# A router stage re-ordered and halved, a last output in two halves, and two norms whose high halves feed TensorE first

## The reference

```
for i in range(DEPTH):                       # DEPTH = 2
    h = pool_mixer(x, ...) if i % 2 == 0 else nsa_mixer(x, ...)
    x = layer_norm(ALPHA * x + h, ln_g[i, 0], ln_b[i, 0])
    f = swiglu(x, ffn_w_gu, ffn_w_down) if i % 2 == 0 else moe_ffn(x, moe_router, moe_w_gu, moe_w_down)
    x = layer_norm(ALPHA * x + f, ln_g[i, 1], ln_b[i, 1])

def moe_ffn(x, router, w_gu, w_down):        # 8 experts, the best 2 of each token, weights by softmax
    top_v, top_i = lax.top_k(x @ router, 2)
    w = softmax(top_v)
    for e in range(8):
        y = y + combine[:, e:e + 1] * swiglu(x, w_gu[e], w_down[e])
```

## Time and profile before

| | |
|---|---|
| median of 3 executions | 2326.48 us |
| lowest and highest | 2321.36 and 2332.45 us |
| the profiled execution, its own time | 2330.26 us |
| its span in the profile | 2328.3 us |
| mean granted TensorE clock | 0.992 |
| busy: TensorE, VectorE, ScalarE | 98%, 81%, 57% |
| expert 0's first slot begins at | 1322.33 us |
| the last expert's last slot ends at about | 2307.9 us |

### The profile page before, as it was taken

The page is one execution under the profiler, slowest core; times in us unless marked ns, Lnnn a source line. Parts: engine busy times, 40 slices in busy tenths (PEclk is TensorE's granted clock), DMA queues, the critical chain, the costliest instruction groups (busy, mean ns, idle before and its releaser), DMA issues.

```text
span 2328.3 us, 35730 instructions
## 1 busy us (share of the span) xinstructions
PE 2281.9 (98%) x14752; PEld 2055.5 (88%) x14752; DVE 1891.2 (81%) x2054; ACT 1322.5 (57%) x1321; POOL 2.4 (0%) x8
## 2 busy tenths in 40 slices
PE   9999999999999999999999999999999999999998
PEld 9799999989989999999987888888888888888886
DVE  7896987787869978645666779898898989898886
ACT  6544343554444434433436377767776777777775
POOL 0000000000000000000000000000000000000000
PEclk9999999999999999999999899999999999999999
DMA  6343445533434553655330399999999999999996
GB/s 264 109 168 136 169 181 182 186 130 117 167 129 177 181 181 127 229 181 182 124 122 9 120 336 374 358 342 368 359 369 363 345 360 373 358 343 356 374 359 257
DMA packets 169552, 556.75 MB, mean 239 GB/s; under 512 B 8752, under 2 KB 8880, under 8 KB 133168
## 3 DMA queue, kind: packets, MB, share of 16 engines
q1 hardware_dynamic: 168048, 547.44, 64.4%
q10 hardware_dynamic: 1152, 6.50, 0.7%
q0 software_dynamic: 192, 0.52, 0.1%
HBM read 552.86 MB, written 1.05 MB: 238 GB/s over the span
## 4 chain that ended last, share of the span: by engine, by line
PE 88%; DVE 6%; ACT 3%; issue 1%; DMA 1%; ACTq 0%; SPq 0%; DVEq 0%
PE ps L1135 14%; PE ps L1137 14%; PE ps L1136 13%; PE ps L1129 12%; PE ps L1131 12%; PE ps L1130 12%; PE ps L1318 2%; ACT whi L628 1%; DMA raw<-stream 1%; DVE wlo L1973 1%; PE ps L1600 1%; PE ps L1797 1%; PE ps L1340 1%; PE ps L1399 1%; PE ps L1421 1%
## 5 line engine op out<-in xcount | busy, mean ns | idle before, releaser
L1973 DVE TENSOR_TENSOR wlo<-raw,whi 128x2048 fp32r<-128x2048 f32 x513 | 1172.1, 2289 | 238.5 <-ACT whi L628 183.2
L628 ACT ACTIVATE whi<-raw 128x2048 fp32r<-128x2048 f32 x513 | 982.3, 1916 | 540.5 <-PE ps L1131 289.8
L1129 PE MATMUL ps<-hh,whi 128*128 128x256 f32 x1920 | 549.0, 286 | 8.1 <-DVE hl L2156 2.1
L1130 PE MATMUL ps<-hl,whi 128*128 128x256 f32 x1920 | 543.8, 283 | 0.0
L1131 PE MATMUL ps<-hh,wlo 128*128 128x256 f32 x1920 | 543.8, 283 | 0.0
L1135 PE MATMUL ps<-whi,hh 128*128 128x512 f32 x960 | 385.6, 402 | 2.0 <-DVE hl L2913 2.0
L1129 PEld LDWEIGHTS ps<-hh,whi 128*128 128x128 f32 x1920 | 369.0, 192 | 11.6 <-issue 6.9
L1137 PE MATMUL ps<-wlo,hh 128*128 128x512 f32 x960 | 377.3, 393 | 0.0
L1136 PE MATMUL ps<-whi,hl 128*128 128x512 f32 x960 | 376.3, 392 | 0.0
L1130 PEld LDWEIGHTS ps<-hl,whi 128*128 128x128 f32 x1920 | 369.1, 192 | 0.3
L1131 PEld LDWEIGHTS ps<-hh,wlo 128*128 128x128 f32 x1920 | 368.9, 192 | 0.0
(11 more groups left out here) (382 smaller groups left out, 2558.3 us busy)
## 6 DMA issues: line engine op xcount, KB each, us to landing
raw<-stream SPq DMA_DIRECT2D x519, 1024.0 KB, 5.5
work<-w_in ACTq DMA_DIRECT2D x1, 2240.0 KB, 9.8
stage<-stage_consts ACTq DMA_DIRECT2D x4, 512.0 KB, 4.0
work<-mem_in ACTq DMA_DIRECT2D x2, 1024.0 KB, 5.4
x<-x_in SPq DMA_DIRECT2D x1, 1024.0 KB, 5.2
out<-x SPq DMA_DIRECT2D x4, 256.0 KB, 2.3
const<-consts SPq DMA_DIRECT2D x1, 548.5 KB, 12.0
work<-work POOLq DMA_DIRECT2D x4, 128.0 KB, 2.8
```

What stands on the lines that cost most here:

```text
L628: nc.scalar.activation(whi[hi_at(g, odd)][:, :], raw[g % RAWS][:, :], ACT.Copy).then_inc(hi_ready, 1)
L1129: mm(out_ap, hi_w, hi_x, start=start, stop=False, **kw)
L1130: mm(out_ap, hi_w, lo_x, start=False, stop=False, **kw)
L1973: V.tensor_tensor(wlo[g % RAWS][:, :], raw[g % RAWS][:, :], whi[hi_at(g, odd)][:, :].bitcast(F32), ALU.subtract).then_inc(lo_ready[g % RAW ...
```

## The change

**Norms 0 and 1.** VectorE now scales all eight blocks and then makes the eight blocks of `hl`. ScalarE follows block by block. The first slot is a new function, `hi_first_slot`: 6 zero matmuls, the wait for the rstd, 2 zero matmuls in place of 16, then 32 matmuls that need only `hh`, each pair of blocks' four as its block is rounded, and last the 16 that need `hl`. Norms 2 and 3 also hand over by block instead of by quarter.

**Router stage.** VectorE's `split_lo(FIRST + AHEAD)` leaves norm 2 and stands between the two kept halves of the gather. Two of the four count products go, and the maximum is taken over the eight columns of places themselves, whose row 0 holds the totals. 10 zero matmuls stand in place of 16. The gather's results are kept and used by halves: expert 0's r = 0, then its r = 1, then the weight half, then expert 1's. TensorE's slot 0 waits for the first half alone. The last four `take_of`, `expert_weights` and the scaling of x move to slots 2, 4 and 8 of expert 0, and `few_give` with the slots' weights to slots 6 and 10.

**The end.** The last down slot takes its matmuls by output half. The high and low half are written by halves, and the first spread needs only the first. 3 zero matmuls stand between the spreads, where 22 stood ahead of them. The table load goes ahead of the last output, the squares and folds move into the branch, and the second half's squares are summed behind the mean.

```diff
+        GIVE_AT = (6, 10)
...
-                for c in range(QUARTERS):
-                    act.wait_ge(norm_scaled, QUARTERS * (SCALED_AT["ln"] + i) + c + 1)
-                    if last:
-                        with_bias(c, x, x_ready)
-                    else:
-                        with_bias(c, hh, hi_done)
+                for b in range(NB):
+                    act.wait_ge(norm_scaled, scaled_block(i, b))
+                    ins = with_bias(b, x if last else hh)
+                    if not last:
+                        ins.then_inc(hi_done, 1)
+                    elif b % 2:
+                        ins.then_inc(x_ready, 1)
...
+                act.wait_ge(y_half_ready, 1)
+                nc.scalar.activation(FEW_Y_HI[:, 0:512], ps[:, 3, :], ACT.Identity, scale=slot_weight(e)).then_inc(y_hi, 1)
+                act.wait_ge(slot_used, SLOTS)
+                nc.scalar.activation(FEW_Y_HI[:, 512:1024], ps[:, 4, :], ACT.Identity, scale=slot_weight(e)).then_inc(y_hi, 1)
...
-                few_keep_y(EXPERTS - 1)
+                load_log_exp()
+                few_keep_last_y()
+                last_squares()
...
+            def hi_first_slot(ph, i, h):
+                g, bank = ph.g, ph.g % BANKS
+                hi, lo = whi[hi_at(g)], wlo[g % RAWS]
+                wait_lo(pe, g)
+                pe.wait_ge(banks_drained, ph.e - 2)
+                keep_warm(bank, 6)
+                pe.wait_ge(rstd_ready, 9 + i)
+                keep_warm(bank, 2)
+                w = lambda t, b, c: t[:, (b * NB + c) * P:(b * NB + c + 1) * P]
+                to = lambda b: ps[:, bank, b * BLK:(b + 1) * BLK]
+                for c in range(NB):
+                    pe.wait_ge(hi_done, rounded_block(i, c))
+                    x_hi = hh[:, c * BLK:(c + 1) * BLK]
+                    for b in range(2):
+                        mm(to(b), w(hi, b, c), x_hi, start=c == 0 and b == 0, stop=False, skip_group_check=True)
+                        mm(to(b), w(lo, b, c), x_hi, start=False, stop=False, skip_group_check=True)
+                for c in range(NB):
+                    if c % 2 == 0:
+                        pe.wait_ge(h_ready, QUARTERS * (h - 1) + c // 2 + 1)
+                    for b in range(2):
+                        last = mm(to(b), w(hi, b, c), hl[:, c * BLK:(c + 1) * BLK], start=False, stop=c == NB - 1, skip_group_check=True)
...
+                squares_of(0)
                 pe.wait_ge(x_folded, 4)
                 ones_sum(MEAN_BANK[3], FOLDED_X[3], False, True).then_inc(mean_ready, 1)
+                squares_of(1)
...
-            ffn_pe(2, 14, norm=8, idle=16)
+            ffn_pe(2, 14)
...
+            hi_first_slot(PHASES["nsa_in"], 1, 15)
...
-            mm(ps[:, 1, 0:8], C("ones"), ind[:, 8:16], start=False, stop=True, skip_group_check=True)
-            mm(ps[:, 1, 16:24], C("ones"), ind[:, 0:8], start=True, stop=False)
-            last = mm(ps[:, 1, 16:24], C("ones"), ind[:, 8:16], start=False, stop=True)
+            last = mm(ps[:, 1, 0:8], C("ones"), ind[:, 8:16], start=False, stop=True, skip_group_check=True)
             last.then_inc(counts_ps, 1)
-            keep_warm(7, 16)
+            keep_warm(7, 10)
...
+                ends = closes and e == EXPERTS - 1
+                order = [(c, b) for b in range(2) for c in range(2)] if ends else [(c, b) for c in range(2) for b in range(2)]
...
+                    if ends and (c, b) == (1, 0):
+                        last.then_inc(y_half_ready, 1)
...
-                pe.wait_ge(gathered, e + 1)
+                if e:
+                    pe.wait_ge(gathered, e + 2)
...
+                        if e == 0 and part == 0 and s < 2:
+                            pe.wait_ge(gathered, s + 1)
...
-                keep_warm(7, 22)
                 pe.wait_ge(y_kept, EXPERTS)
                 few_spread(EXPERTS - 1, 0, 5)
+                keep_warm(7, 3)
+                pe.wait_ge(y_kept, EXPERTS + 1)
                 few_spread(EXPERTS - 1, 1, 3)
...
-                for c in range(QUARTERS + 1):
-                    if c < QUARTERS:
-                        for b in (2 * c, 2 * c + 1):
-                            ins = V.scalar_tensor_tensor(out=xb(b), in0=xb(b), scalar=R("ln_g", g_at + b), in1=rstd[:, :],
-                                                         op0=ALU.mult, op1=ALU.mult)
-                        ins.then_inc(norm_scaled, 1)
-                    if c and not last:
-                        dve.wait_ge(hi_done, QUARTERS * HI_AT[f"ln{i}"] + c)
-                        for b in (2 * c - 2, 2 * c - 1):
-                            cols = slice(b * BLK, (b + 1) * BLK)
-                            ins = V.scalar_tensor_tensor(out=hl[:, cols], in0=xb(b), scalar=R("ln_b", 8 * i + b), in1=hh[:, cols].bitcast(F32),
-                                                         op0=ALU.add, op1=ALU.subtract)
-                        ins.then_inc(h_ready, 1)
+                for b in range(NB):
+                    V.scalar_tensor_tensor(out=xb(b), in0=xb(b), scalar=R("ln_g", g_at + b), in1=rstd[:, :],
+                                           op0=ALU.mult, op1=ALU.mult).then_inc(norm_scaled, 1)
+                if not last:
+                    for b in range(NB):
+                        dve.wait_ge(hi_done, rounded_block(i, b))
+                        cols = slice(b * BLK, (b + 1) * BLK)
+                        ins = V.scalar_tensor_tensor(out=hl[:, cols], in0=xb(b), scalar=R("ln_b", 8 * i + b), in1=hh[:, cols].bitcast(F32),
+                                                     op0=ALU.add, op1=ALU.subtract)
+                        if b % 2:
+                            ins.then_inc(h_ready, 1)
...
-            layer_norm(2, 16, last=True, beside=FIRST + AHEAD)
+            layer_norm(2, 16, last=True)
...
-            step(V.tensor_reduce(small[:, 472:473], ps[:, 1, 16:24], AX, ALU.max))
+            step(V.tensor_reduce(small[:, 472:473], ps[:, 1, 0:8], AX, ALU.max))
...
-                for odd in range(2):
-                    if odd == 0:
-                        dve.wait_ge(gathered_ps, 1)
-                    first = keep_x_hi(0, odd, 5)
-                    if odd == 0:
-                        dve.wait_ge(gathered_ps, 2)
-                    second = keep_x_hi(1, odd, 3)
-                    keep_x_lo(0, odd, 5, first)
-                    keep_x_lo(1, odd, 3, second).then_inc(gathered, 1)
+                def keep_first(r, odd, done=None):
+                    bank = (5, 3)[r]
+                    dve.wait_ge(gathered_ps, r + 1)
+                    lo = keep_x_lo(r, odd, bank, keep_x_hi(r, odd, bank))
+                    if done is not None:
+                        lo.then_inc(done, 1)
+                keep_first(0, 0, gathered)
+                keep_first(1, 0, gathered)
+                split_lo(FIRST + AHEAD)
+                keep_first(0, 1)
+                keep_first(1, 1, gathered)
                 V.memset(small[:, 639:640], 0.0).then_inc(gather_kept, 2)
-                for n in range(12, 16):
-                    ins = take_of(n)
-                ins.then_inc(places_built, 1)
-                V.tensor_scalar(x[:, :], x[:, :], ALPHA, None, ALU.mult).then_inc(y_added, 1)
-                expert_weights()
+                def last_takes():
+                    for n in range(12, 16):
+                        ins = take_of(n)
+                    ins.then_inc(places_built, 1)
+                def scale_x():
+                    V.tensor_scalar(x[:, :], x[:, :], ALPHA, None, ALU.mult).then_inc(y_added, 1)
+                beside_first = {2: last_takes, 4: expert_weights, 8: scale_x}
...
-                few_keep_y_lo(EXPERTS - 1)
+                for half in range(2):
+                    cols = slice(512 * half, 512 * (half + 1))
+                    dve.wait_ge(y_hi, EXPERTS + half)
+                    V.scalar_tensor_tensor(out=FEW_Y_LO[:, cols], in0=ps[:, 3 + half, :], scalar=slot_weight(EXPERTS - 1),
+                                           in1=FEW_Y_HI[:, cols].bitcast(F32), op0=ALU.mult, op1=ALU.subtract).then_inc(y_kept, 1)
...
+                last_folds()
```

91 lines of the change are left out of this document (51 added, 40 removed).

## The result

The changed kernel took 2313.15 us, the median of 8 executions (2311.34 to 2315.35). The kernel before took 2327.81 us beside it (8 executions, 2321.36 to 2334.0). The ratio is 0.9944, with a 95% interval of 0.993 to 0.9959. That is 14.7 us or 0.56% faster, and the interval reaches across the line of 0.5%. A later set of 7 executions of the same changed kernel gave 2313.74 us and a ratio of 0.9952 (0.993 to 0.9973). The forecast was 2315.0 us.

What follows compares the result with a forecast made beforehand. TensorE, busy 2281.9 of 2328.3 us, was taken as the bound; 3.8 + 5.9 + 1.7 - 1.0 + 3.1 + 0.4 = 13.9 us gave 2316.4 from the profile, 2313.4 from the median, middle 2315.0; range 2309 to 2323 us.

Steps and rivals of the forecast that it cites:

- norms 0 and 1: First slots behind both norms: TensorE starts on the first rounded block and ends 1.9 us earlier each, together 3.8 us.
- slot 0 of expert 0, behind norm 2's rstd: Router stage: earlier gather, then no wait for conversions, so slot 0 starts at 1316.4 in place of 1322.33, 5.9 us.
- clock behind the pause: Stretch 1320 to 1330, behind the 1.98 us pause: without a pause the 1.2 GHz loss goes, 1.7 us.
- the wait for `routed`: Expert 0, ahead of the column products: VectorE's moved work ends late and TensorE waits, -1.0 us.
- the end, with norm 3 by block: Behind the last slot: mean at 2314.35 in place of 2317.45, 3.1 us, and norm 3's hand-over by block another 0.4 us.
- Rival (d): Norms 0 and 1: first slots still end with the last `hl` and gain nothing, 2318.8 us; chance 0.05.
- The gather's start: Router stage: the gather starts at 1311.8 in place of 1315.85, 4.05 us, behind VectorE's flag, low half and takes.
- rival (c): Around the gather: the low clock also gets shorter, up to another 3 us won, 2312 us; chance 0.08.
- rival (b): Expert 0: VectorE's queue runs late, up to 6.4 us less won, 2321.4 us; chance 0.10.
- The prediction's own alternative: At the end: were the instruction fetch stall behind the branch twice as long, the 3.1 us would be 2.0.
- Rival (a): Norms 0 and 1: TensorE's pauses bring 1.2 GHz stretches; one fall gives 2316.7 us, both 2318.4; chance 0.30.
- Rival (e): Norms, router and end: long 1.2 GHz stretches cost 20.9 us, slower than before at 2335.9 us; chance 0.02.

Runs made afterwards that it cites:

- the end alone: The kernel before with only the change's part at the end (output halves, 3 zeros, table load, folds and squares in the branch): 2324.09 us, ratio 0.9996.
- its own run: The changed kernel with the low weight half made at the end of norm 2 again, as in the kernel before: 2316.94 us.
- the norms alone: The kernel before with only the norms' part (high halves first behind norms 0 and 1, hand-over by block in all four norms): 2323.95 us, ratio 0.998.
- the gather whole: The changed kernel with the gathered x kept as before, slot 0 of expert 0 waiting for both halves: 2314.23 us.
- the router part alone: The kernel before with only the router stage's part (weight half, counts, zeros, gather by halves, moved work): 2320.55 us, ratio 0.9976.
- The run with the norm in the branch: The changed kernel with norm 3 of VectorE and ScalarE written inside both branches of the experts: 2313.28 us, ratio 0.9958.

## Why the prediction was right, point by point

The forecast of 2315.0 us is 1.9 us above the first median and 1.3 above the second. 11.6 us (0.5%) was the line between faster and no change. The medians lie 3.1 and 1.1 us past it, but both intervals reach back across it, so the measurement leaves open which of the two it is; the prediction had given 0.40 to faster and 0.58 to no change.

| step | forecast, us | profile before to profile after, us |
|---|---|---|
| norms 0 and 1 | 3.8 | 1.88 + 1.87 = 3.75 |
| slot 0 of expert 0, behind norm 2's rstd | 5.9 | 22.40 - 15.82 = 6.6 |
| clock behind the pause, less the wait for `routed` | 1.7 - 1.0 = 0.7 | slot 0 to last slot 985.5 - 983.2 = 2.3 |
| the end, with norm 3 by block | 3.1 + 0.4 = 3.5 | 20.47 - 17.91 = 2.6 |
| places that the change leaves alone | 0 | norm 1 to norm 2's rstd 3.2, ahead of norm 0 0.5 |
| sum | 13.9 | 18.9 |

- **Norms: right, with its mechanism.** First matmul 1.54 us behind the rstd (1.4 forecast); the part alone gives the same. Rival (d) falls.
- **The gather's start: the changed row as forecast, the gain (4.02 us against 4.05) in part by luck.** Logits' end to gather is 6.22 us, the forecast 6.3. But the forecast set this against rows of before that were partly at 1.2 GHz (1.73 us for the count products and 3.76 us for 16 zeros, at a clock of 0.65), as if they were the kernel's own. Against the same stage with the same 1.7 us lost (the end alone) the gain is 2.25 us: the weight half's (1.7 to 2.4 us by its own run) and norm 2's hand-over by block (0.3 to 0.4). The other 1.8 us are clock: before lost 1.6 + 3.5 us from 1300 to 1320, after 0.6 + 1.1 us from 1290 to 1310. The cut products and zeros bring nothing at the full clock. The forecast had TensorE's zeros (1311.5) and VectorE's takes (1311.8) nearly level; VectorE comes 0.93 us later.
- **Slot 0: the mechanism right, its size too large.** No idle time there; from the first transpose 10.28 us (10.9 forecast, 16.5 before), and the halves give 2.1 us by their own run. The gather takes 3.92 us and not 4.6, at a higher clock. But at equal lost time the stage gains 4.4 us, not 5.9 (4.1 if the 16.12 of the changed kernel's second profile is taken, which lost 1.7 us there too); the 6.6 of the table has 2.2 us of clock in it. This is rival (c) in part: it had the low clock get shorter.
- **The stretch behind the pause of 1.98 us** was gone, but it need not have been there. The pause stood in four profiles (before, the norms alone, the end alone, the gather whole), and only before had the clock fall right behind it. Of the 2.3 us in the table 1.7 are the clock (3.4 us lost in before from slot 0 on, 1.7 in after), and the rest goes with TensorE's waits in the experts, which come to 3.5 us in before and 2.7 in after.
- **`routed`: oversized.** 0.24 us in after (0.47 with the router part alone), not 1.0. No wait for a weight half stood in expert 0, so rival (b) falls.
- **The end: the step that failed.** The mean came 6.40 us behind the last slot, as forecast. But "a stall as long as these rows have it" was the wrong size. The 1.24 and 1.30 us of `issue` are only what showed of the stall behind work that covered its start; from fetch to next instruction it is 1.5 to 2.0 us in both kernels. In after the engines' next work comes 1.89 us behind the last square and 2.31 behind the last fold, and so stands 0.39 and 1.03 us later behind the mean than in before. The run with the norm in the branch has both gone. That is most of the 0.9 us by which this row misses its forecast. The Trainium skill ("Runtime: NRT & Kernel Launch", "Instruction fetch mechanics") says that a taken branch to code outside the fetched pages waits for a fetch. The trace agrees: the stall was moved, not removed, and queue 14 has a fetch behind each engine's last instruction ahead of the jump. The prediction's own alternative, 2.0 us for a stall twice as long, is near the 2.25 of the end alone.
- **Rival (a)** didn't show in the first profile and did in the second, at norm 0. At 3 of 16 places and 1.7 us each that is some 0.6 us an execution (an estimate), not the 1.7 or 3.4 of the rival. Without the zeros both norms had it in the one profile taken. **Rival (e)** never came near.
- **What the sum can't hold:** 3.7 of the 18.9 us lie where no line was changed. The 3.2 us between norms 1 and 2 are clock: before lost 5.1 us there and after 1.7.
- **Why the number came out all the same.** At equal clock the rows give 3.75 + 4.4 + 2.6 us less the 0.24 of `routed`, some 10.5 us, where the forecast had 12.2 without its clock term. The clock made up the difference. By the mean clocks of all executions with one on record, 67 of before lost 14.4 us and 15 of after 11.7 in the mean (an estimate: what the clock misses to 1, times the span), with a standard error of 1.2 us on the difference. So some 2.7 us of clock go with the changed kernel, where the forecast counted 0.85 to 1.7 behind one pause. That oversized gains and an undersized clock term cancelled is luck. Taking the median of before rather than its profiled execution was not.
